# A dense last stage for tiles 6, 7 and the samples of a PEER layer, with six tiles still gathered

## The reference

```
q = norm(h) @ w_peer_q                       # 8 heads, two halves of 128
s1, s2 = q_half @ sub_keys (128 each)        # top 16 of either half
cand = v1[:, None] + v2[None, :]             # 256, of which the top 16 again
eidx = e1 * 128 + e2 ; g = softmax(score)    # 8 x 16 = 128 experts a token
act = gelu(expert_u[eidx] . x)
out = h + sum(g * act * expert_v[eidx])
```

## Time and profile before

| what | us |
|---|---|
| median of 3 runs (lowest, highest) | 4226.0 (4222.43, 4232.14) |
| profiled execution, span from the first to the last instruction | 4221.9 |
| its wave 0 ends at about (tiles 0 and 1 named) | 612 |
| its waves 1 to 4 end at about (samples named) | 3955 |

### The profile page before, as it was taken

How to read it: one execution, slowest core, us unless ns; L and a number is a source line. 1 busy time by engine, 2 the same in 40 slices (tenths; PEclk the granted TensorE clock), 3 DMA queues, 4 the chain that set the end, 5 groups by cost and what they waited for, 6 DMA issues and landing times.

```text
span 4221.9 us, 32194 instructions
## 1 busy us (share of the span) xinstructions
PE 3201.1 (76%) x9766; PEld 1661.7 (39%) x9766; DVE 2854.8 (68%) x5552; ACT 1198.4 (28%) x2584; POOL 1367.6 (32%) x1086
## 2 busy tenths in 40 slices
PE   6989918869887677859887759997586677768565
PEld 3345613325445333425454424554262233334222
DVE  2012285778767966768766978886889767467865
ACT  1223102126521112126631116664111245111100
POOL 0000011444433322433333324443434333434463
PEclk9976959878888878978888878998798788878777
DMA  3422346999999958998989888999999888999997
GB/s 122 138 69 102 113 174 229 401 401 384 382 401 380 369 198 304 410 373 353 345 359 392 316 301 347 379 386 383 380 398 364 302 333 339 400 418 384 383 419 324
DMA packets 296027, 1367.21 MB, mean 324 GB/s; under 512 B 36056, under 2 KB 96624, under 8 KB 149392
## 3 DMA queue, kind: packets, MB, share of 16 engines
q0 software_dynamic: 154464, 1116.02, 66.1%
q1 hardware_dynamic: 110480, 222.78, 14.8%
q10 hardware_dynamic: 30912, 26.35, 1.9%
HBM read 1329.52 MB, written 35.10 MB: 323 GB/s over the span
## 4 chain that ended last, share of the span: by engine, by line
DVE 22%; DMA 12%; PE 11%; ACT 5%; issue 5%; SPq 2%; POOL 1%; ACTq 0%; DVEq 0%; POOLq 0%
DVE uv L1365 10%; DMA uv<-expert_uv,rows_u 8%; PE pv L796 5%; DVE held L1388 2%; SPq L537 2%; DVE arena L1356 1%; PE pb L906 1%; DMA uv<-expert_uv,rows_pk 1%; DMA arena<-scratch_gates 1%; POOL uv L699 1%; PE pb L854 1%; PE pb L749 1%; ACT L1140 1%; PE pb L879 1%; DVE arena L1426 1%
## 5 line engine op out<-in xcount | busy, mean ns | idle before, releaser
L699 POOL DMA_INDIRECT uv<-expert_uv,rows_u x1024 | 1311.7, 1281 | 2203.1 <-PE pv L796 1225.8
L796 PE MATMUL pv<-uv,diag 128*128 128x512 f32 x2344 | 1263.8, 696 | 404.2 <-ACT diag L1102 329.5
L1365 DVE CUSTOM_DVE_ANT_0 uv<-uv,nr 128x1024 f32<-128x1024 f32 x1056 | 1240.8, 1220 | 195.5 <-DMA uv<-expert_uv,rows_u 160.9
L796 PEld LDWEIGHTS pv<-uv,diag 128*128 128x128 f32 x2344 | 511.4, 226 | 1062.0 <-issue 984.0
L965 PE MATMUL pb<-arena 128*128 128x512 f32 (+1 forms) x1440 | 651.9, 611 | 35.5 <-ACT arena L1249 35.5
L1388 DVE SCALAR_TENSOR_TENSOR held<-uv,wgt,held 128x1024 f32<-128x1024 f32 x470 | 603.9, 1285 | 16.6 <-DVE wgt L1376 0.3
L1109 ACT ACTIVATE gel<-dots 128x4 f32<-128x4 f32 x264 | 54.2, 205 | 1878.3 <-DVE dots L1365 1810.2
L965 PEld LDWEIGHTS pb<-arena 128*128 128x128 f32 (+1 forms) x1440 | 266.6, 189 | 398.4 <-issue 357.5
L749 PE MATMUL pb<-arena 64*128 64x512 f32 (+6 forms) x544 | 274.1, 621 | 166.2 <-DMA arena<-scratch_c_p 94.2
L778 PE MATMUL pb<-arena 128*128 128x64 f32 (+3 forms) x1728 | 248.7, 290 | 35.2 <-ACT o L1091 35.2
L778 PEld LDWEIGHTS pb<-arena 128*128 128x128 f32 (+3 forms) x1728 | 229.9, 197 | 102.1 <-issue 66.3
(11 more groups left out here) (149 smaller groups left out, 2631.3 us busy)
## 6 DMA issues: line engine op xcount, KB each, us to landing
arena<-w_stream SPq DMA_DIRECT2D x80, 1024.0 KB, 9.3
arena<-w_main SPq DMA_DIRECT2D x60, 1024.0 KB, 9.5
uv<-expert_uv,rows_u POOLq DMA_INDIRECT x1024, 10.9
scratch_gates<-arena ACTq DMA_DIRECT2D x32, 256.0 KB, 9.7
arena<-scratch_gates SPq DMA_DIRECT2D x8, 1024.0 KB, 22.2
o<-x SPq DMA_DIRECT2D x14, 512.0 KB, 15.1
arena<-scratch_c_p SPq DMA_DIRECT2D x8, 520.0 KB, 8.2
arena<-x_t SPq DMA_DIRECT2D x8, 512.0 KB, 5.6
```

The lines of the kernel that those rows point to most:

```text
L699: pool.indirect_dma_start(out=uv[k % NU][:].rearrange("p a n -> p (a n)"), out_offset=None, in_=io["expert_uv"][:, :], in_offset=bass.Indi ...
L796: mm = nc.tensor.matmul(pv[:, c * BANK:(c + 1) * BANK], diag[n % ND][:], uv[k % NU][:, 1, c * BANK:(c + 1) * BANK], start=n == first, stop ...
L1365: nc.vector.tensor_tensor_reduce(out=u, in0=u, in1=row[:], scale=1.0, scalar=0.0, op0=ALU.mult, op1=ALU.add, accum_out=dots[b % 2][:, k % ...
```

## The change

Six tiles (0 to 5) stay gathered, 192 lots in all. Waves 1 to 4 carry 44, 44, 30 and 10 of them, and the last 64 (tiles 4 and 5) run inside a new last stage, all their sums on VectorE. Tiles 6, 7 and the samples, 288 tokens, take all 16384 experts densely in that stage:

- Where a dense tile's experts are named, its two halves e1 and e2 and the gates go to memory (`picks`), its normed rows turned go to `xd`.
- The stage loads the picks, turns them (tokens become columns), and makes a table of gates: for each token a product of two one-hot matrices, 128 picks by 128 keys, gives the gate of each of 128 x 128 experts. Four tokens are a group (72 groups), 32 tokens a strip (9 strips), which is stored to memory.
- Then come 128 blocks of 128 experts. A block's scores are 8 products of a turned block of u with the 288 tokens' columns; ScalarE takes the gelu, VectorE multiplies by the block's strip of the table. Four blocks (a "super") later, 8 groups of 4 products with v sum into PSUM, and VectorE adds each to `acc`. Every other block carries a dot of one gathered lot, the block behind it its sums.
- The sums are turned back, added to h and stored.

The stretches of the merge that change beside this: the normed rows are made in the buffer `mt` of the merged rows (so that the norm waits for `h_ready` of both tiles), stored to memory, and loaded again on POOL's queue into two buffers `nr` when their tile's gathers begin. `expert_u_t`, the u rows turned by blocks, is an argument that is laid out beforehand.

```diff
-LEFT = 16
+GATHERED = 6
+DENSE = tuple(range(GATHERED, TILES))
+WD = P * (len(DENSE) - 1) + NS
+STRIP = 32
+STRIPS = WD // STRIP
+GROUP = 4
+GROUPS = WD // GROUP
+SUPER = 4
+SUPERS = NK // SUPER
+NUB = 4
+NWT = 3
+DLOTS = 64
+BUDGET = (0, 44, 44, 30, 10)
...
-            first = self.tiles[g - 1][0] * LOTS
-            count = self.tiles[g][0] * LOTS - first - (0 if g < len(WAVES) - 1 else LEFT)
+            first = sum(BUDGET[:g])
+            count = BUDGET[g]
...
+            self.dots_in[i * NK // DLOTS] = b
+            self.sums_in[i * NK // DLOTS + 1] = b
...
@@ on SP @@
+                def load_u(e):
+                    if e >= NUB:
+                        sp.wait_ge(s_done, e - NUB + 1)
+                    sp.dma_start(ub[e % NUB].rearrange("p k n -> p (k n)"), io["expert_u_t"][e]).then_inc(u_in[e % NUB], 16)
+                def load_v(s):
+                    if s >= 2:
+                        sp.wait_ge(v_done, KD * (s - 1))
...
+                def load_weights(s):
+                    if s >= NWT:
+                        sp.wait_ge(v_done, KD * (s - NWT + 1))
...
+                    for n in range(STRIPS):
+                        sp.wait_ge(tab_out, STRIP // GROUP * (n + 1))
+                        sp.dma_start(dram["table"][n * P:(n + 1) * P, :], strip[n % 2].rearrange("p e t -> p (e t)")).then_inc(strip_stored[n % 2], 16)
+                    sp.wait_ge(strip_stored[0], 16 * ((STRIPS + 1) // 2))
+                    sp.wait_ge(strip_stored[1], 16 * (STRIPS // 2))
+                    load_weights(0)
+                    load_v(0)
...
+                        if t < GATHERED:
+                            sp.wait_ge(nr_ready, t + 1)
+                            sp.dma_start(dram["n2"][first_row(t):first_row(t) + r, :], nrow[ti][0:r]).then_inc(n2_stored, 16)
...
@@ on POOL @@
+                        pool.wait_ge(dotted, slots_to(t - 2))
+                    pool.dma_start(nr[t % 2][0:r], dram["n2"][first_row(t):first_row(t) + r, :]).then_inc(nr_in[t % 2], 16)
...
@@ on PE @@
+                def table(n):
+                    pe.wait_ge(hot_made, n + 1)
+                    if n >= 3:
+                        pe.wait_ge(tab_out, n - 2)
+                    for j in range(GROUP):
+                        mm = nc.tensor.matmul(pb[:, 3 + n % 3, j * P:(j + 1) * P], hot_col[n % 2][:, j, :], hot_row[n % 2][:, j, :],
+                                              start=True, stop=True)
+                    mm.then_inc(tab_made, 1)
+                def dense_scores(e):
+                    pe.wait_ge(u_in[e % NUB], 16 * (e // NUB + 1))
+                    if e >= 2:
+                        pe.wait_ge(s_gelu, e - 1)
+                    for k in range(KD):
+                        mm = nc.tensor.matmul(pb[:, e % 2, 0:WD], ub[e % NUB][:, k, :], xd[:, k, :], start=k == 0, stop=k == KD - 1)
+                    mm.then_inc(s_done, 1)
+                def dense_values(s, dc):
+                    n = s * KD + dc
+                    if dc == 0:
+                        pe.wait_ge(v_in[s % 2], 16 * (s // 2 + 1))
+                        pe.wait_ge(w_ready, SUPER * (s + 1))
+                    if n >= 4:
+                        pe.wait_ge(added, n - 3)
+                    for b in range(SUPER):
+                        mm = nc.tensor.matmul(pb[:, 2 + n % 4, 0:WD].rearrange("p (g t) -> p g t", t=STRIP),
+                                              vb[s % 2][:, b, dc * P:(dc + 1) * P], wt[s % NWT][:, :, b, :], start=b == 0, stop=b == SUPER - 1)
+                    mm.then_inc(v_done, 1)
+                def dense():
...
+                    for e in range(NK + SUPER):
+                        if e < NK:
+                            dense_scores(e)
+                        if e >= SUPER:
+                            for dc in range(2 * (e % SUPER), 2 * (e % SUPER) + 2):
+                                dense_values(e // SUPER - 1, dc)
+                    turn_sums_back()
...
@@ on ACT @@
-                            if t >= 3:
-                                act.wait_ge(dotted, slots_to(t - 3))
-                            row = nr[t % 3][0:r]
+                            act.wait_ge(h_ready, 2 * (tiles[-1] + 1))
+                            row = nrow[ti][0:r]
...
+                    for n in range(GROUPS):
+                        i, j = n // (STRIP // GROUP), n % (STRIP // GROUP)
+                        act.wait_ge(tab_made, n + 1)
...
+                        nc.scalar.activation(strip[i % 2][:, :, j * GROUP:(j + 1) * GROUP],
+                                             pb[:, 3 + n % 3, :].rearrange("p (t e) -> p e t", t=GROUP), ACT.Copy).then_inc(tab_out, 1)
...
@@ on DVE @@
+                def hots(n):
+                    if n >= 2:
+                        dve.wait_ge(tab_made, n - 1)
+                    cols = slice(n * GROUP, (n + 1) * GROUP)
+                    for j in range(GROUP):
+                        i = n * GROUP + j
+                        nc.vector.tensor_scalar(hot_row[n % 2][:, j, :], iota[:], et[:, 0, i:i + 1], et[:, 2, i:i + 1], ALU.is_equal, ALU.mult)
+                    nc.vector.tensor_tensor(hot_col[n % 2], et[:, 1, cols].unsqueeze(2).to_broadcast([P, GROUP, P]),
+                                            iota[:].unsqueeze(1).to_broadcast([P, GROUP, P]), ALU.is_equal).then_inc(hot_made, 1)
...
+                    nc.vector.tensor_tensor(w, w, gl[e % 2].rearrange("p (g t) -> p g t", t=STRIP), ALU.mult).then_inc(w_ready, 1)
...
+                        nc.vector.tensor_tensor(acc[:, dc, :], acc[:, dc, :], pb[:, 2 + n % 4, 0:WD], ALU.add).then_inc(added, 1)
...
+                    for e in range(NK + SUPER):
+                        if e < NK:
+                            weigh_block(e)
+                        if e in plan.sums_in:
+                            weigh(plan.sums_in[e])
+                        if e in plan.dots_in:
+                            dot(plan.dots_in[e])
+                        if e >= SUPER:
+                            for dc in range(2 * (e % SUPER), 2 * (e % SUPER) + 2):
+                                add_block(e // SUPER - 1, dc)
```

More of the change, by code:

```diff
@@ L255, in __init__ @@
                     self.kind_of[b] = kind if g < len(WAVES) - 1 else "samples"
-        self.rest = range(SAMPLES * LOTS - LEFT, ALL_SLOTS // LOT)
+        self.before = sum(BUDGET)
+        assert self.before + DLOTS == ALL_SLOTS // LOT
+        self.dots_in, self.sums_in = {}, {}
+        for i in range(DLOTS):
+            b = self.before + i
+            self.kind_of[b] = "dense"
+            self.dots_in[i * NK // DLOTS] = b
+            self.sums_in[i * NK // DLOTS + 1] = b
     def on_dve(self, k):
@@ L404, in stream @@
         assert at[0] <= ARENA - D
+        at[0] = 0
+        ub = [carve(KD, P) for _ in range(NUB)]
+        vb_at = at[0]
+        vb = [carve(SUPER, D) for _ in range(2)]
+        acc_at = at[0]
+        acc = carve(KD, WD)
+        xd = carve(KD, WD)
+        wt_at = at[0]
+        wt = [carve(STRIPS, SUPER, STRIP) for _ in range(NWT)]
+        gl = [carve(WD) for _ in range(2)]
+        hd = [o_rows[i][:].rearrange("p k n -> p (k n)") for i in range(2)] + [carve(D)]
+        at[0] = vb_at
+        strip = [carve(NK, STRIP) for _ in range(2)]
+        at[0] = acc_at
+        hot_row = [carve(GROUP, P) for _ in range(2)]
+        hot_col = [carve(GROUP, P) for _ in range(2)]
+        assert at[0] <= acc_at + KD * WD
+        at[0] = wt_at
+        pk = [carve(3, NK) for _ in DENSE]
+        et = carve(3, WD)
+        assert at[0] <= wt_at + NWT * STRIPS * SUPER * STRIP
         pv = ctx.enter_context(nc.psum_tensor("pv", [P, D], F32))
@@ L724, in _ @@
                     if j == 0:
[L725 to L728, removed]
+                        pool.wait_ge(named, t + 1)
                         load_tile(t)
@@ L798, in background, with turn_picks @@
                         mm.then_inc(valued, 1)
[L800 to L805, removed]
-                                              start=True, stop=True)
-                    mm.then_inc(folded, 1)
+                def turn_picks():
+                    pe.wait_ge(pk_in, 16 * len(DENSE))
+                    for i, t in enumerate(DENSE):
+                        r, col = query_rows(t), dense_col(t)
+                        for c in range(3):
+                            mm = nc.tensor.transpose(pb[:, c, col:col + r], pk[i][0:r, c, :], ident[0:r, 0:r])
+                    mm.then_inc(pk_turned, 1)
@@ L1030, in _ @@
                     merge(g)
[L1031 to L1034, removed]
+                dense()
             @block.scalar
```

233 lines of the change are left out of this document (171 added, 62 removed).

## The result

The changed kernel takes 4462.9 us (median of 4 runs, 4461.1 to 4471.7) against 4224.2 for the one before (4 runs, 4219.8 to 4232.1): ratio 1.0567, 95% interval 1.0551 to 1.0584, so 239 us slower. The forecast was 4629, 403 us slower: the sign was right, and 164 us of the slowdown did not come.

What follows compares the result with a forecast made beforehand. The prediction held the waves bound by transfers and compute almost equally: 4221.9 - 267 (last stretch) - 622 (waves) + 12 (added wait) + 1280 (dense stage) = 4625, so 4629 us as median; 8-in-10 range 4430 to 4820.

Steps and rivals of the forecast that it cites:

- Rival 1: Transfers bound the waves: each removed lot gives 11.1 us, total 4008 us, faster; chance 0.05.
- six fewer in each give 21 + 31 = 52: Projecting, waves 1 and 2: 18 to 12 lots each, at 3.5 and 5.1 us a lot, saves 52 us.
- Attending: Attending in waves 1 to 4: fewer TensorE slots at 1.72 us save 31, 31, 72, 77, plus 35; 246 us.
- The 35 us of wave 4's wait for keys and values: Attending in wave 4: of 46 us waiting for keys and values behind the gathers, 35 come back.
- rival 3: TensorE's clock falls in attending with fewer lots; if half of 337 us comes, total 4800; chance 0.14.
- half the slots' price, 111: Attending's lower bound: 111 us saved if VectorE or the chain of a unit is next.
- Merging: Merging in waves 1 to 4: fewer lots save 33, 33, 103 and 155, sum 324 us.
- Added wait and stores: Waves: first norm waits for both tiles' products, 12 us; stores and reload of normed rows cost nothing.
- The stage: New last stage: way in 15, table 120, turn-round 10, loop 1100, way out 35; sum 1280 us.
- 400 throughout: Dense loop's transfers, 421.5 MB: at 400 GB/s throughout 1054 us; with SP's 153 MB at 357, 1100.
- the likeliest case: Whole kernel: the forecast itself, 4629 us, own range 4540 to 4720; chance 0.53.
- rival 2: Both sides better: merges at 7.9 us a lot (+103), loop 1075, table 111; total 4490; chance 0.14.

## Why the forecast was right in sign and too high

- **The argument holds.** The break-even by the rows was 9.15 us a lot, by measurement 8.4; the lots gave 6.3 (forecast 5.55). Rival 1 would have needed 11.1, and the waves ended at 3249, not before 2900.
- **The mis-sized step is projecting:** "six fewer in each give 21 + 31 = 52". By its own cuts it gave 304 - 245 + 333 - 257 = 135, 83 of the 164 us. A straight line per lot was wrong: the first twelve cost 4 and 16 us, the last six 59 and 76. The stretches of the earlier trace rows also held the turn to attending, with its wait for the reloaded forget sums. The forecast priced such a wait in wave 4 alone; in waves 1 and 2 it fell from 64.4 to 20.6 us, and of it 56 and 6.5 us lie inside the cuts of projecting, which makes some 50 of the 135. Another 73 are in the columns, mostly transfers by the run without them, and 13 lie ahead of the first product.
- **Attending:** forecast 246, measured 39 + 27 + 61 + 96 = 223. The 123 slots gave 1.8 us each in the mean, near the 1.72 of the forecast. The 35 us of wave 4's wait for keys and values did not come: TensorE waited 46.2 us there before and 45.7 after. The clock fell from 0.86 to 0.75 in wave 3 and from 0.77 to 0.59 in wave 4, the mild form of rival 3; what that cost is not shown. Below 15 lots it went on: wave 3 bare is 340 us. The lower bound, "half the slots' price, 111", is 106 by its own terms; the forecast itself does not rest on it.
- **Merging:** forecast 324, measured 39 + 40 + 97 + 175 = 351. Wave 3's own slope, 5.6, was right (5.7); wave 4's lots were worth 7.6, near the upper slope of 7.9, not the middle.
- **Added wait and stores:** forecast 12 and nothing; 10 net together, by the run with the old load in waves 1 to 3.
- **The stage:** forecast 1280, measured 1212. The way in took 14 (15), the table 120 (120), with VectorE busy 117 of it as the step said. DMA was not "nearly idle" there, 0.44: the table's own stores run. Loop, turn-round and way out were put at 1145 and took 1078. The loop's 1066 lies near the 1054 of "400 throughout" rather than the 1100 taken, and the way out took 12, not 35. That transfers and not TensorE set it was right, by a small distance: 1066 against 1007. The Trainium skill's 358 GB/s at the memory side ("DMA: Bandwidth & Descriptors", "Where 436 GB/s comes from") would have made the loop 1177 us, as an estimate; it ran at 388 GB/s.
- **Sum:** the waves gave 99 us more than forecast, the stage cost 68 less, and wave 0 took 3 more: that is the 164.
- **The range:** 4463 lies below the likeliest case's own 4540 to 4720; it is in the wider 4430 to 4820 because that took in rival 2, whose 4490 came nearest. Rival 2's loop came (1066 for 1075), but its merges gave 27 of the 103 us; what brought the time down to it was projecting, which it doesn't name. So far the hit is luck.

## What to carry to other kernels

A lot's price depends on where it stands: 0.9 us in a loop bound nearly as much by compute, 4 to 8 in a merge, 1.1 to 3.6 in wave 3's attending, 0.2 to 1.3 for the first twelve and then 6 beside projecting's columns, 11.1 alone. Take the price from two lengths of the same stage with different loads, look for where the line bends, and check whether the stretch holds a wait at its edge that isn't the stage's own. Before moving work out of a full pipeline into a stage of its own, work out that stage empty: here it cost over 1100 us with nothing hidden in it, more than all that was taken away, while moving six lots a wave to a neighbouring stage gave 1%.

## What the runs showed of the hardware

- Attending without lots held the granted clock at 0.50 although its matmul records covered 319 of 340 us; two idle products of 384 columns a unit brought it to 0.88 and shortened the stage. In wave 0's attending one a unit left 0.51 and made the stretch 41 us longer; two brought 0.95, and it was still 11 us longer.
- With one core running, transfers held 388 GB/s over 1066 us, gathers and large loads together.
- With the DMA engines 0.97 to 0.98 busy, taking 216 us of work off TensorE turned into 224 us more of waiting for u's loads.
- At the turn from projecting to attending the last store of 256 KB and the reload behind it took some 13 and 8 us to land with the DMA engines fully busy, and about 4 each at a share of 0.67.
